# Sum units in the first block of the up projections of a fused RG-LRU / MLA decoder trunk

## The reference, cut to what matters

```python
SEQ, D_MODEL, D_FF = 256, 2048, 5632

def swiglu(hn, w_in, w_out):
    u = hn @ w_in                                              # (256, 2048) @ (2048, 11264)
    return (jax.nn.silu(u[..., :D_FF]) * u[..., D_FF:]) @ w_out

for layer in range(DEPTH):                                     # DEPTH = 2
    ...
    h = h + swiglu(rmsnorm(h, norm_ffn[layer]), ffn_w_in[layer], ffn_w_out[layer])
```

## Time and profile before

| | us |
|---|---|
| median of three runs | 1967.86 (1967.45 to 1967.99) |
| the profiled execution, its own time | 1967.33 |
| its span, first to last instruction | 1965.5 |
| TensorE matmul busy | 1957.2 (100%) |
| VectorE busy | 1713.6 (87%) |
| ScalarE busy | 1163.6 (59%) |
| GpSimd busy | 153.4 (8%) |

### The profile page before, as it was taken

One profiled execution on the slowest core, in us unless ns is written; L12 is line 12 of the kernel. 1 busy time (PEld: TensorE's weight loads), 2 busy tenths in 40 slices (PEclk: granted clock), 3 DMA queues, 4 the chain that ended last, 5 costly groups with the idle time before them and its releaser, 6 DMA issues.

```text
span 1965.5 us, 23834 instructions
## 1 busy us (share of the span) xinstructions
PE 1957.2 (100%) x9348; PEld 1646.3 (84%) x9348; DVE 1713.6 (87%) x1931; ACT 1163.6 (59%) x1465; POOL 153.4 (8%) x143
## 2 busy tenths in 40 slices
PE   9999999999999999999999999999999999999999
PEld 8898888888888888888898888888888888888887
DVE  7979846899999999999976886479999999999997
ACT  5488545656565556666666664555565565566563
POOL 1000210010001101000002110000001100010000
PEclk9999999999999999999999999999999999999999
DMA  8664663566666666666564335456666666666664
GB/s 283 207 200 161 225 215 129 194 204 200 196 208 198 206 199 196 209 195 203 182 223 147 114 127 194 143 178 208 198 206 201 197 201 202 204 202 200 204 198 148
DMA packets 160685, 378.62 MB, mean 193 GB/s; under 512 B 6298, under 2 KB 11172, under 8 KB 160452
## 3 DMA queue, kind: packets, MB, share of 16 engines
q1 hardware_dynamic: 160276, 376.06, 57.9%
q0 software_dynamic: 272, 1.13, 0.2%
q10 hardware_dynamic: 32, 0.01, 0.0%
HBM read 375.08 MB, written 2.10 MB: 192 GB/s over the span
## 4 chain that ended last, share of the span: by engine, by line
PE 92%; issue 5%; DVE 1%; POOL 1%; ACT 0%; DMA 0%; POOLq 0%; SPq 0%; ACTq 0%
PE bank L1935 78%; PE bank L2133 6%; PE bank L2131 3%; PE bank L1896 2%; PE bank L1928 1%; PE bank L2117 1%; PE bank L1919 1%; DVE w_lo L1120 0%; POOL stats L1877 0%; PE bank L2130 0%; DMA raw<-in_lru_w_in 0%; ACT w_hi L654 0%; POOL stats L1875 0%; PE bank L2097 0%; POOL stats L1873 0%
## 5 line engine op out<-in xcount | busy, mean ns | idle before, releaser
L1935 PE MATMUL bank<-w_hi,act 128*128 128x512 f32 x3440 | 1104.3, 390 | 0.0
L1935 PEld LDWEIGHTS bank<-w_hi,act 128*128 128x128 f32 x3440 | 645.7, 188 | 133.5
L1935 PE MATMUL bank<-raw_lo,act 128*128 128x512 f32 x1464 | 569.9, 389 | 0.0
L654 ACT ACTIVATE w_hi<-raw 128x2048 fp32r<-128x2048 f32 (+1 forms) x240 | 448.5, 1882 | 155.6 <-PE bank L1935 66.4
L1935 PEld LDWEIGHTS bank<-raw_lo,act 128*128 128x128 f32 x1464 | 274.9, 188 | 56.5
L1120 DVE TENSOR_TENSOR raw_lo<-raw,w_hi 128x2048 fp32r<-128x2048 f32 x116 | 264.0, 2286 | 21.3 <-ACT w_hi L654 21.1
L731 ACT ACTIVATE w_lo<-t_raw 128x1024 fp32r<-128x1024 f32 x108 | 114.2, 1058 | 272.8 <-DVE t_raw L1177 272.8
L1190 DVE TENSOR_TENSOR raw_lo<-raw,w_hi 128x2048 fp32r<-128x2048 f32 x108 | 246.6, 2283 | 0.0
L1120 DVE TENSOR_TENSOR w_lo<-raw,w_hi 128x2048 fp32r<-128x2048 f32 (+1 forms) x84 | 183.1, 2190 | 64.2 <-ACT w_hi L654 63.9
L1935 PE MATMUL bank<-w_lo,act 128*128 128x512 f32 x580 | 190.8, 389 | 0.0
L2133 PE MATMUL bank<-act,w_hi 128*128 128x512 f32 x480 | 169.0, 396 | 0.0
(11 more groups left out here) (247 smaller groups left out, 2365.7 us busy)
## 6 DMA issues: line engine op xcount, KB each, us to landing
raw<-in_ffn_w_in SPq DMA_DIRECT2D x176, 1024.0 KB, 5.4
raw<-in_ffn_w_out SPq DMA_DIRECT2D x88, 1024.0 KB, 5.3
raw<-in_lru_w_in SPq DMA_DIRECT2D x28, 1024.0 KB, 5.5
raw<-in_lru_w_out SPq DMA_DIRECT2D x16, 1024.0 KB, 4.9
raw<-in_w_o SPq DMA_DIRECT2D x16, 1024.0 KB, 5.5
raw<-in_w_ukv SPq DMA_DIRECT2D x8, 1024.0 KB, 5.4
raw<-in_w_uq SPq DMA_DIRECT2D x8, 768.0 KB, 4.6
raw<-in_w_dkv SPq DMA_DIRECT2D x8, 576.0 KB, 4.3
```

What stands on the lines that cost most here:

```text
L654: A.activation(flat_chunk(w_hi, SLOT[c], size), flat_chunk(raw, SLOT[c], size), ACT.Copy).then_inc(w_hi_done, 1)
L1935: i = T.matmul(bank[:, :], x_part, w_part, start=first and n == 0, stop=last and n == 2)
```

## The change

Block 0 of each up projection gets two sum units, 5 and 6 (`EARLY_SUMS`), and is otherwise run by the same loops as the other blocks on each engine: its results are combined through the shared banks (banks 4 to 7), Silu reads `gtmp`, and GpSimd makes half of the low parts of the first two chunks of block 1. TensorE waits for `side_lo` at unit 5 of block 0, and at unit 0 of block 1 for the shared adds of block 0. The steps at which the activation sums, their high and their low parts are made (2, 3 and 4) stay. ScalarE gets a Silu of one column at its step 2. The counts that semaphores wait for are adapted.

```diff
+EARLY_SUMS = (5, 6)
 FIRST_SUM, LAST_SUM = 2, 6
+def sums_of(i):
+    return UP_SUMS if i else EARLY_SUMS
-SUM_BLOCKS = S_BLOCKS + 2
-POOL_UNITS = 2 * S_BLOCKS
-UP_TOTAL = SIDES * S_BLOCKS
+SUM_BLOCKS = FB + 2
+POOL_UNITS = 2 * FB
+UP_TOTAL = len(EARLY_SUMS) + SIDES * S_BLOCKS
...
 # ScalarE
+            def table(func):
+                A.activation(stat(TABLE_SLOT), minus_half[:, 0:1], func)
...
-                for u in range(8):
-                    if u == 1:
-                        act_tiles(d, 3)
-                    if u == 3:
-                        act.wait_ge(side_done, f + 1)
-                        A.activation(s_hi, side[:, 0:SIDE_SETS, :, :], ACT.Copy)
-                        A.activation(side_last[:, 0, :, :], side[:, SIDE_SETS, :, :], ACT.Copy).then_inc(side_hi, 1)
-                    if u == 7:
-                        act.wait_ge(chunk_used, c0 + 8)
-                        act.wait_ge(rstd_done, d + 1)
-                        for t in range(NT):
-                            k = silu(t, ps[2 * t][:, :])
-                        k.then_inc(silu_done, 1)
-                    following(0, u)
-                for i in range(1, FB):
+                for i in range(FB):
                     shared = banks_of(i % 2 == 1)[1]
                     for u in range(8):
-                        if u == 0:
+                        if i and u == 0:
                             gT_out(i - 1, i + FB * f, shared[0:2])
+                        if i == 0 and u == 1:
+                            act_tiles(d, 3)
+                        if i == 0 and u == 2:
+                            act.wait_ge(consts, 1)
+                            table(ACT.Silu)
+                        if i == 0 and u == 3:
+                            act.wait_ge(side_done, f + 1)
+                            A.activation(s_hi, side[:, 0:SIDE_SETS, :, :], ACT.Copy)
+                            A.activation(side_last[:, 0, :, :], side[:, SIDE_SETS, :, :], ACT.Copy).then_inc(side_hi, 1)
...
                         if u == 7:
+                            if i == 0:
+                                act.wait_ge(rstd_done, d + 1)
...
 # VectorE
-                    elif i > 1 and u < 2:
+                    elif i and u < 2:
                         split_half(c)
-                    elif i and u in UP_SUMS:
+                    elif u in sums_of(i):
...
-                    if u == 6:
-                        sums(c0 + 8 + FIRST_SUM, unit_no(f, 1, FIRST_SUM), UP_PLACE[FIRST_SUM])
-                        continue
-                    if u == 7:
-                        dve.wait_ge(chunk_used, c0 + 8)
-                        dve.wait_ge(silu_done, FB * f + 1)
-                        gated(0, ps[1][:, :])
-                        gated(1, ps[3][:, :]).then_inc(g_done, 1)
-                        following(0, 6)
-                    following(0, u)
-                for i in range(1, FB):
+                for i in range(FB):
                     result, shared = banks_of(i % 2 == 1)
                     for u in range(8):
+                        if i == 0 and u == 1:
+                            act_tiles(d, 3)
+                        if i == 0 and u == 2:
+                            make_sides()
+                        if i == 0 and u == 4:
+                            sides_low()
...
                         if u == 6:
-                            shared_add(shared, i + (SUM_BLOCKS * f - 1), i + (FB + 2) * f)
+                            shared_add(shared, i + SUM_BLOCKS * f, i + (FB + 2) * f)
...
 # GpSimd, low_halves
-                for i in range(1, FB):
+                for i in range(FB):
...
 # TensorE
-                for u in range(8):
-                    pe.wait_ge(act_lo_done, LO0[d] + max(8, 2 * u + 2))
-                    pe.wait_ge(w_lo_done, c0 + u + 1)
-                    plain_unit(c0 + u, 2 * u, ps[0:4], u == 0, u == 7).then_inc(chunk_used, 1)
-                    if u < 2:
-                        transpose_h(d, 2 + u)
-                for i in range(1, FB):
+                for i in range(FB):
                     result, shared = banks_of(i % 2 == 1)
+                    first = sums_of(i)[0]
                     for u in range(8):
                         c = c0 + 8 * i + u
-                        if u == 0:
+                        if i == 0:
+                            pe.wait_ge(act_lo_done, LO0[d] + max(8, 2 * u + 2))
+                        elif u == 0:
                             pe.wait_ge(u_done, i + (FB + 2) * f)
-                        if i == 1 and u == FIRST_SUM:
+                        if i == 0 and u == first:
                             pe.wait_ge(side_lo, f + 1)
...
-                        if u in UP_SUMS:
-                            e = sum_unit(c, UP_PLACE[u], UP_SUMS.index(u), 2 * u, result, shared, u == FIRST_SUM,
+                        if u in sums_of(i):
+                            e = sum_unit(c, UP_PLACE[u], UP_SUMS.index(u), 2 * u, result, shared, u == first,
                                          u == LAST_SUM, i + FB * f)
-                        elif u < 2:
+                        elif i and u < 2:
...
+                        if i == 0 and u < 2:
+                            transpose_h(d, 2 + u)
```

More of the change, by code:

```diff
@@ L244, in build_program @@
         NMX, PSUMS, RPS = 50, 54, 58
-        SS_KR4, QK_EPS4, INV_QK4, WAIT_SLOT, POOL_SLOT = 64, 68, 72, 76, 77
+        SS_KR4, QK_EPS4, INV_QK4, WAIT_SLOT, POOL_SLOT, TABLE_SLOT = 64, 68, 72, 76, 77, 78
         x_in = [sem(f"x_in{b}") for b in range(NB)]
@@ L594, in unit_no @@
         def unit_no(f, i, u):
-            return SUMS * f + SIDES * (i - 1) + UP_SUMS.index(u)
+            before = len(EARLY_SUMS) + SIDES * (i - 1) if i else 0
+            return SUMS * f + before + sums_of(i).index(u)
         def half_tiles(c, part):
@@ L604, in pool_lo_needed @@
         def pool_lo_needed(f, i, u):
-            return 2 * i + (POOL_UNITS * f + u - 3)
+            return POOL_UNITS * f + 2 * (i - 1) + u + 1
         def side_parts(j):
@@ L1293, in shared_to_h @@
                     n = 4 * f + 2 * half
-                    shared_add(banks_of(half == 0)[1], SUM_BLOCKS * f + S_BLOCKS + half,
+                    shared_add(banks_of(half == 0)[1], SUM_BLOCKS * f + FB + half,
                                (FB + 2) * f + FB + half)
@@ L1333, in following @@
                         down_split(f, u)
-                    elif i > 1 and u < 2:
+                    elif i and u < 2:
                         split_half(c)
-                    elif i and u in UP_SUMS:
+                    elif u in sums_of(i):
                         if u != FIRST_SUM:
-                            user = [v for v in range(u - SLOTS + 1, u) if UP_PLACE.get(v) == UP_PLACE[u]]
+                            user = [v for v in sums_of(i) if u - SLOTS < v < u and UP_PLACE[v] == UP_PLACE[u]]
                             sums(c, unit_no(f, i, u), UP_PLACE[u], behind=c0 + 8 * i + user[0] + 1 if user else None)
@@ L1351, in result_out @@
                     k.then_inc(r_done, 1)
-                    dve.wait_ge(r_done, i + S_BLOCKS * f)
+                    dve.wait_ge(r_done, i + (FB * f + 1))
                     dve.wait_ge(silu_done, i + (FB * f + 1))
@@ L1389, in up, with make_sides @@
-                for i in range(1, FB):
+                def make_sides():
+                    dve.wait_ge(side_copied, SIDES * (f + 1))
+                    a11, a21 = side_a[:, :, 0, 0:P], side_a[:, :, 0, P:SEQ]
+                    a12, a22 = side_a[:, :, 1, 0:P], side_a[:, :, 1, P:SEQ]
+                    V.tensor_tensor(side[:, :, 0, :], a22, a21, ALU.subtract).then_inc(u_side, 1)
+                    V.tensor_tensor(side[:, :, 2, :], a11, a21, ALU.subtract)
+                    dve.wait_ge(u_side, 2 * f + 1)
+                    V.scalar_tensor_tensor(out=side[:, :, 1, :], in0=side[:, :, 0, :], scalar=-1.0, in1=a11,
+                                           op0=ALU.mult, op1=ALU.subtract).then_inc(u_side, 1)
+                    dve.wait_ge(u_side, 2 * f + 2)
+                    V.tensor_tensor(side[:, :, 3, :], a12, side[:, :, 1, :], ALU.add).then_inc(side_done, 1)
@@ L1390, in up, with sides_low @@
+                def sides_low():
+                    dve.wait_ge(side_hi, f + 1)
+                    V.tensor_tensor(s_lo, side[:, 0:SIDE_SETS, :, :], s_hi.bitcast(F32), ALU.subtract)
+                    V.tensor_tensor(side_last[:, 1, :, :], side[:, SIDE_SETS, :, :],
+                                    side_last[:, 0, :, :].bitcast(F32), ALU.subtract).then_inc(side_lo, 1)
+                for i in range(FB):
                     result, shared = banks_of(i % 2 == 1)
                     for u in range(8):
+                        if i == 0 and u == 1:
[4 more added lines that the diff above has]
+                            sides_low()
@@ L1842, in low_halves @@
                         if u == 0:
-                            pool.wait_ge(p1_done, i + SUM_BLOCKS * f)
```

(7 more changed lines are left out.)

3 lines of the change are left out of this document (1 added, 2 removed).

## The result

The changed kernel takes 1986.43 us (median of 6 runs, 1985.3 to 1988.89) against 1967.65 before (1967.36 to 1967.99). The ratio is 1.0097, 95% interval 1.0087 to 1.0108: 18.8 us slower. 1986.5 was forecast. The profiled execution took 1985.66 us, its span is 1983.7.

What follows compares the result with a forecast made beforehand. TensorE, busy 1957.2 of 1965.5 us, was taken as the bound. Per projection 8.5 - 1.36 + 2.2 = 9.3 us, two 18.7, on 1967.33 gives 1986.0, plus 0.5 for the median: 1986.5, range 1981.2 to 1989.8.

Steps and rivals of the forecast that it cites:

- The order of the steps: VectorE's queue after the activation tiles in block 0: unit 5, sums, unit 6, unit 7's split, low parts at 341.5.
- steps 1 to 3 of VectorE: Unit 5's weights to 327.2, activation sums to 329.8, unit 6's weights to 336.3, unit 7's plain split to 339.1.
- ScalarE's hand-over: At step 3 VectorE waits for ScalarE before unit 7's plain split, idle for 0.6 us.
- the prediction's own sign: Stated test: the prediction is wrong in a term if VectorE's idle wait for ScalarE at step 3 is not 0.6 us.
- The stall: TensorE waits at unit 5 of block 0 for side_lo, 341.5 against 333.0: 8.5 us in each projection.
- The matmuls: Two sum units of 21 instead of 24 matmuls in block 0 save 1.36 us a projection.
- What follows the stall: After the wait VectorE is idle, not behind; shared adds, GpSimd halves and Silu from SBUF cost 0.
- Rival 3: A second wait behind the stall, in blocks 0 and 1, up to 1.3 us a projection: 1989.1 us; chance 0.09.
- The restart: After the wait at unit 5 TensorE resumes at half clock: 2.2 us a projection, between 0 and 2.8.
- Rival 1: The same wait at unit 5, but the clock stays, no slow restart: 1982.1 us; chance 0.22.
- rival 2: Sums ready before TensorE's unit 5 at 333.0, only the 2.7 us saving left: 1965.1 us; chance 0.04.

Runs made afterwards that it cites:

- wait_only: Kernel before the change, with only TensorE's wait for side_lo moved to unit 5 of block 0: 1970.76 us, ratio 1.0017.
- low_step3: Changed kernel with the low parts of the activation sums made at VectorE's step 3 instead of step 4: 1981.74 us, ratio 1.0070.
- sides_first: Changed kernel with the activation sums and their high parts at step 1, low parts at step 2, ahead of unit 6: 1971.72 us, ratio 1.0020.
- only_unit6: Changed kernel with one sum unit in block 0, unit 6, instead of units 5 and 6: 1966.74 us, ratio 0.9993.
- two_sets: Changed kernel with only the activation sums for units 5 and 6 made early (VectorE steps 1 and 2), the others at steps 3 and 4: 1967.43 us.

## Why the prediction was right

**The order of the steps.** It said that steps 1 to 3 of VectorE run to 339.1 and side_lo comes at 341.5. The rows are 338.95 and 341.3. The preparation of unit 5 ended at 327.13 (327.2 in the working), the sums at 329.67 (329.8), unit 6 at 336.2 (336.3). ScalarE's hand-over was 0.47 us, not 0.6: by the prediction's own sign a wrong term, of 0.13 us.

**The stall.** 8.5 us from matmul to matmul; the last matmul started at 332.74 and the next was due 0.23 later, at 332.97, so it was 341.41 - 332.97 = 8.44, in the second projection 8.4. wait_only shows the part that the place of the wait has, low_step3, sides_first and only_unit6 that the rest follows the queue.

**The matmuls.** 1.36 us a projection is right, seen in the chain (174 instead of 180). As time it is seen only in part where nothing stalls: 1.2 us a projection up to block 1 in two_sets, before VectorE took it back.

**What follows the stall.** No second wait, as said: VectorE is idle for 9.99 us and every later block takes its 41.8 us. Rival 3 falls.

**The restart.** 2.2 us a projection were taken, between 0 and 2.8. The two profiles of the changed kernel give 25.13, 25.05, 26.26 and 25.63 us for the 102 matmuls, against 23.54 with the array kept busy: 1.5 to 2.7, mean 2.0. Rival 1 falls: the clock does fall. By the rule of the Trainium skill ("TensorE: Matmul & The Clock Gate", Part 1, The HAM clock gate), that an array without work falls back to half clock, the loss was certain, and it came at all four holes. That 2.2 lies so near is in part luck: it came from transposes at the start of the run, where the clock reads 1.00, and no run shows that they and these matmuls are slow for one reason.

**The hit and the small errors.** 1986.5 against 1986.43 is luck below 1 us: the same kernel's second median is 1987.46. The stalls and the saving give 14.1 of the 18.8 us, the restarts 4.0; some 0.7 is left over, half of which is 0.03 us more in each block of the second projection, not an effect of the sum units, as wait_only has it too. The working put the lower end of rival 1 at 1980.9, and the range begins at 1981.2 without a reason; nothing hung on it. And rival 2 was put too simply: "the sums are ready in time, only the saving is left" is two statements. two_sets made the first true, and the saving was lost again in block 1.

## What to carry to other kernels

When work is brought forward, look for everything that it needs and find where each of those stands in its engine's queue; here the engines' step numbers stayed and one wait moved 28 us ahead of them. Add up the whole queue between the producer's last free moment and the new due time, then do the same for the next few users, since a queue that is just in time for the new unit is late for those behind it. A saving of TensorE time is worth it only where the engine that feeds it has idle time left in the same stretch: here, in the orders that were run, VectorE had room for one sum unit in block 0, not for two.

## What the runs showed of the hardware

- Waits of TensorE of 5.5 and 8.3 us brought its clock from 1.00 to 0.50 in all six places seen (changed kernel in two profiles, low_step3), and cost 1.4 to 2.7 us on top of the wait. Waits of 1.0 to 1.6 us (sides_first, wait_only) left it at 1.00.
- What the restart costs differs from run to run for the same wait: 25.05 to 26.26 us for the same 102 matmuls, with the clock back 3.2 to 5.8 us after they begin.
- 34 matmuls without use in each hole are worth 2.0 to 2.5 us a projection.
- GpSimd operations on SBUF about doubled the time of VectorE operations with both sources in SBUF that ran beside them (4.08 against 1.95 us, 0.79 to 0.96 against 0.42).
